# Strassen's block scheme for the up projections of two feed-forwards, with the feed-forward in two phases

## What is computed

```
def conv_ffn(h, w_up, conv_w, conv_b, w_down):
    u = h @ w_up                                  # 528x1024 @ 1024x5632
    up = jnp.pad(u, ((0, 0), (CONV_W - 1, 0), (0, 0)))
    c = conv_b + sum(up[:, j:j + Tp] * conv_w[j] for j in range(CONV_W))   # CONV_W = 3
    gate, val = jnp.split(c, 2, axis=-1)
    return (jax.nn.silu(gate) * val) @ w_down     # 528x2816 @ 2816x1024
h = h + conv_ffn(rms_norm(h, ln_ffn_g[i]), w_up[i], conv_w[i], conv_b[i], w_down[i])
```

## Time and profile before

| | |
|---|---|
| median of 3 runs (lowest, highest) | 2502.92 us (2499.54, 2505.1) |
| profiled execution: span, first to last instruction | 2497.3 us |
| PE, weight loads, DVE, ACT, POOL busy | 2391.5, 2135.3, 1371.9, 1060.1, 397.6 us |
| mean granted TensorE clock, as a share of full | 0.979 |
| `f0u`, `f0d` (us from the start) | 1375 to 1633, 1633 to 1762 |
| `f1u`, `f1d` | 2104 to 2362, 2362 to 2486 |

### The profile page before, as it was taken

The page is one execution under the profiler, slowest core; times in us unless marked ns, Lnnn a source line. Parts: engine busy times, 40 slices in busy tenths (PEclk is TensorE's granted clock), DMA queues, the critical chain, the costliest instruction groups (busy, mean ns, idle before and its releaser), DMA issues.

```text
span 2497.3 us, 41318 instructions
## 1 busy us (share of the span) xinstructions
PE 2391.5 (96%) x15443; PEld 2135.3 (86%) x15443; DVE 1371.9 (55%) x2095; ACT 1060.1 (42%) x1910; POOL 397.6 (16%) x350
## 2 busy tenths in 40 slices
PE   6999999999999999998989999999999989999998
PEld 5778777887899899887869999999888879999987
DVE  5896777223465245458745666643334445766621
ACT  5646764333343233324444333332455554333322
POOL 0000444700410100100121211100100002211100
PEclk8999999999999999999989999999999999999999
DMA  8563423332233353332102323323422122232332
GB/s 291 166 205 103 109 77 84 93 101 81 88 96 92 100 134 87 101 110 65 44 19 66 91 86 90 92 85 93 131 60 60 45 52 85 84 92 85 89 95 92
DMA packets 409481, 238.38 MB, mean 95 GB/s; under 512 B 11434, under 2 KB 400397, under 8 KB 409381
## 3 DMA queue, kind: packets, MB, share of 16 engines
q1 hardware_dynamic: 400549, 202.25, 28.8%
q0 software_dynamic: 8224, 32.61, 3.9%
q10 hardware_dynamic: 608, 2.16, 0.2%
HBM read 234.54 MB, written 5.00 MB: 96 GB/s over the span
## 4 chain that ended last, share of the span: by engine, by line
PE 81%; DVE 6%; ACT 5%; issue 4%; DMA 3%; POOL 0%; SPq 0%; ACTq 0%; DVEq 0%; POOLq 0%
PE PS L508 60%; PE PS L2056 6%; PE PS L1842 3%; DMA w_raw<-in_w_in_dram 2%; ACT w_hi L429 1%; PE PS L2092 1%; PE PS L1857 1%; PE PS L2187 1%; PE PS L1801 1%; DVE w_lo L435 1%; PE PS L1921 1%; PE PS L2134 1%; PE PS L1957 1%; PE PS L2071 1%; DVE conv_acc L2311 1%
## 5 line engine op out<-in xcount | busy, mean ns | idle before, releaser
L435 DVE TENSOR_TENSOR w_lo<-w_raw,w_hi 128x1024 fp32r<-128x1024 f32 (+2 forms) x376 | 470.4, 1251 | 628.4 <-ACT w_hi L429 627.3
L508 PE MATMUL PS<-op_hi,w_hi 128*128 128x264 f32 (+3 forms) x2440 | 600.9, 310 | 16.3 <-DVE w_lo L435 13.6
L508 PE MATMUL PS<-op_lo,w_hi 128*128 128x264 f32 (+3 forms) x2440 | 598.4, 309 | 0.0
L508 PE MATMUL PS<-op_hi,w_lo 128*128 128x264 f32 (+3 forms) x2440 | 595.8, 308 | 0.0
L429 ACT ACTIVATE w_hi<-w_raw 128x1024 fp32r<-128x1024 f32 (+2 forms) x376 | 378.9, 1008 | 314.0 <-PE PS L508 261.6
L508 PEld LDWEIGHTS PS<-op_hi,w_hi 128*128 128x128 f32 x2440 | 397.1, 189 | 47.7 <-DVE w_lo L435 16.3
L508 PEld LDWEIGHTS PS<-op_hi,w_lo 128*128 128x128 f32 x2440 | 396.7, 189 | 22.6
L508 PEld LDWEIGHTS PS<-op_lo,w_hi 128*128 128x128 f32 x2440 | 396.2, 189 | 21.9 <-issue 0.5
L508 PE MATMUL PS<-ff_hi,w_lo 128*128 128x512 f32 (+1 forms) x784 | 240.3, 343 | 0.0
L508 PE MATMUL PS<-ff_hi,w_hi 128*128 128x512 f32 (+1 forms) x784 | 239.9, 342 | 0.0
L508 PE MATMUL PS<-ff_lo,w_hi 128*128 128x512 f32 (+1 forms) x784 | 239.9, 342 | 0.0
(11 more groups left out here) (497 smaller groups left out, 3856.7 us busy)
## 6 DMA issues: line engine op xcount, KB each, us to landing
w_raw<-in_w_up_dram SPq DMA_DIRECT2D x120, 512.0 KB, 3.8
w_raw<-in_w_in_dram SPq DMA_DIRECT2D x64, 512.0 KB, 4.1
w_raw<-in_w_down_dram SPq DMA_DIRECT2D x64, 512.0 KB, 3.8
w_ada<-in_w_ada_dram POOLq DMA_DIRECT2D x12, 2048.0 KB, 9.0
decay<-sums_scratch SPq DMA_DIRECT2D x16, 512.0 KB, 5.2
w_raw<-in_w_branch_ssd_dram SPq DMA_DIRECT2D x16, 512.0 KB, 4.0
w_raw<-in_w_in_a_dram SPq DMA_DIRECT2D x16, 512.0 KB, 3.8
w_raw<-in_w_kv_b_dram SPq DMA_DIRECT2D x16, 512.0 KB, 3.9
```

What stands on the lines that cost most here:

```text
L435: dve.tensor_tensor(wlo[slot][:, 0:ks, :], wraw[slot][:, 0:ks, :], whi[slot][:, 0:ks, :].bitcast(F32), ALU.subtract).then_inc(sem("w_split ...
L508: last = pe.matmul(a[0:l.cols, h, 0:cn], w[slot][:, k, 0:l.cols], x[:, kk, c0:c0 + cn], start=(j == 0 and k == 0 and w is whi and x is l.h ...
```

## The change

The two `f{x}u` are replaced by a block scheme. A gate tile and a value tile of the weights form, with the two halves of the contraction (4 tiles each), a 2 by 2 block matrix; the activations form one with the contraction's halves and the token halves. The 8 block products become 7, each of 4 contraction tiles, 3 passes and 264 columns: 84 matmuls a pair. In exchange sums of blocks are formed. Of the activations this happens once a layer, in `to_feed_forward`: the second token half of `op_hi`, `op_lo` is now a difference of the halves, and there are three combined blocks `tx_val`, `tx_hi`, `tx_lo`. Of the weights it happens for every pair: POOL makes 4 sums (`fs_sum`), ACT 7 hi parts (`fs_hi`), DVE 7 lo parts (`fs_lo`). Sums of products are formed by ACT copying one PSUM bank into another before PE adds on to it, and by 2 additions on DVE.

Other parts of it: the feed-forward goes in phases of 12 and 10 tile pairs (`PHASE`), with a part of the down projection (`f{x}d0`, 12 contraction tiles; `f{x}d1`, 10) behind each; the first tap of the convolution moves from DVE to ACT, gate times value from DVE to POOL; after the last down projection DVE adds from PSUM, where ACT copied and POOL added. In the rest of the program some semaphores share a name; its work is the same.

```
+PHASE = 12
+        for ph in range(2):
+            L[f"f0d{ph}"] = Linear(plan, KD, down_src(I["w_down_2"][0], PHASE * ph), GHs[0], GLs[0],
+                                  kts=((8, 4), (8, 2))[ph], block1=False)
 # POOL, weights: four sums a pair
+            def fs_sums(x, t, par, i):
...
+                if not first:
+                    p = (5, 6, 7, 3)[i]
...
+                    pool.wait_ge(sem("fs_done"), fs_at(x, t, par, 7, place - 7))
+                if i == 0:
+                    pool.wait_ge(sem(f"fs_in{par}"), t * 32 + 32 * (NF // 2 * x + 1))
+                    a, b, op = raw[1][:, 0:4, :], raw[1][:, 4:8, :], ALU.add
+                elif i == 1:
...
+                    a, b, op = fs_sum[0][:], raw[0][:, 0:4, :], ALU.subtract
+                elif i == 2:
+                    a, b, op = raw[0][:, 0:4, :], raw[1][:, 0:4, :], ALU.subtract
+                else:
...
+                    a, b, op = raw[0][:, 4:8, :], fs_sum[1][:], ALU.subtract
+                pool.tensor_tensor(fs_sum[i][:], a, b, op).then_inc(sem("fs_sum"), 1)
 # POOL, one pair
+                def body(t, par, conv=True, ahead=True):
...
+                        fs_sums(x, nt, np_, 0)
+                        fs_sums(x, nt, np_, 1)
+                    if conv:
+                        gated(pt, pp)
+                    if ahead:
+                        fs_sums(x, nt, np_, 2)
+                        fs_sums(x, nt, np_, 3)
...
+                    scale(t, par, 0)
+                    scale(t, par, 1)
 # PE, one pair
+                    for p in (1, 5, 2, 6, 7, 3, 4) if first else (1, 5, 6, 2, 7, 3, 4):
+                        pe.wait_ge(sem("fs_lo"), fs_at(x, t, par, 7, FS_LO_NO[p]))
+                        if p in FS_SEED:
+                            pe.wait_ge(sem("fs_seed"), fs_at(x, t, par, 3, FS_SEED[p]))
...
+                        for k in range(4):
...
+                            for n, (w, v) in enumerate(((FS_HI[p], hi), (FS_HI[p], lo), (FS_LO[p][par], hi))):
+                                last = pe.matmul(acc, w[:, k, :], v[:, k, :], start=(p in (1, 5) and k + n == 0),
+                                                 stop=(k == 3 and n == 2), skip_group_check=True)
 # DVE, the lo part of product p's weights; one pair
+            def fs_lo(p, x, t, par):
+
+                dve.wait_ge(sem("fs_hi"), fs_at(x, t, par, 7, FS_HI_NO[p]))
+                if p in (5, 6, 2):
+                    dve.wait_ge(sem("fs_sum"), fs_at(x, t, par, 4, 2 if p == 5 else 4))
+                dve.tensor_tensor(FS_LO[p][par][:], fs_raw_of(p, par), FS_HI[p][:].bitcast(F32),
+                                  ALU.subtract).then_inc(sem("fs_lo"), 1)
 # DVE, operands, for each of the 8 residual tiles
+                    if g >= 4:
+                        k = g - 4
+                        link(dve.scalar_tensor_tensor(tv[:, 1, k, :], R[:, g, TH:T], gain(g), tv[:, 1, k, :], ALU.mult,
+                                                      ALU.subtract))
+                        link(dve.scalar_tensor_tensor(tv[:, 0, k, :], R[:, k, 0:TH], gain(k), tv[:, 1, k, :], ALU.mult,
+                                                      ALU.add))
+                        dve.scalar_tensor_tensor(tv[:, 2, k, :], R[:, g, 0:TH], gain(g), tv[:, 0, k, :], ALU.mult,
+                                                 ALU.subtract).then_inc(sem("fs_tv"), 1)
+                    if g >= 5:
+                        t_lo(g - 5)
+                    for p in {6: (1,), 7: (5,)}.get(g, ()):
+                        fs_lo(p, x, 0, 0)
```

More of the change, by code:

```diff
@@ L406, in halves, with load @@
             return ap.rearrange("p (a n) -> p a n", a=2)
-        def load(sp, l):
+        def load(sp, l, start=0):
             def body(g, t, par):
@@ L420, in load @@
             else:
-                pair_loop(sp, None, 0, l.groups, body)
+                for g in range(start, start + start % 2):
+                    body(g, g // 2, g % 2)
+                pair_loop(sp, None, start + start % 2, l.groups, body)
         def split_hi(act, l, t, par, j, ks=8):
@@ L492, in products_of @@
             cols = [(META, S)] if l.block1 else [(0, TH), (TH, TH)]
-            if l.hi is not HH and l.hi is not GH and l.block1:
+            if l.block1 and not any(l.hi is b for b in (HH, *GHs)):
                 cols = [(0, S)]
@@ L594, in late_sum @@
             return between
[L596 to L604, removed]
-            pair_loop(pool, None, 0, L[name].groups, body)
         def attn_gain(k):
@@ L928, in decay_rows, with fs_load @@
                 sp.dma_start(decay[i % 2][:], src).then_inc(sem(f"decay_in{i % 2}"), 16)
+            def fs_load(x, t, par):
+                w = I["w_up_2"][x].rearrange("(k p) n -> p k n", p=P)
+                first = isinstance(t, int) and t == 0
+                for u in range(2):
+                    if not first:
+                        if u:
+                            sp.wait_ge(sem("fs_lo"), fs_at(x, t - 1, par, 7, FS_LO_NO[4]))
+                        else:
+                            sp.wait_ge(sem("fs_done"), fs_at(x, t - 1, par, 7, FS_PLACE[2]))
+                    src = w[:, :, bass.ds(t * (2 * P) + (par * P + u * FF2), P)]
+                    sp.dma_start(fs_raw[par][u][:], src).then_inc(sem(f"fs_in{par}"), 16)
             for name, l in L.items():
@@ L1111, in _ @@
+            resid_sum_ff(0, "n4", L["oa2"])
+            for ph in range(2):
+                fs_pool(0, ph)
             link(pool.memset(stats[:], 1.0))
@@ L1513, in _, with fs_hi @@
-            feed_forward(0, "n4")
-            gained_hi(act, "n6", lambda k: attn_gain(KD + k), QHh, ("evacuated", L["f0d"].G0 + KD + 2))
+            def fs_hi(p, x, t, par):
+                if p in (1, 4):
+                    act.wait_ge(sem(f"fs_in{par}"), t * 32 + 32 * (NF // 2 * x + 1))
+                elif p != 2:
+                    act.wait_ge(sem("fs_sum"), fs_at(x, t, par, 4, FS_SUM[p] + 1))
+                act.activation(FS_HI[p][:], fs_raw_of(p, par), ACT.Copy).then_inc(sem("fs_hi"), 1)
@@ L2043, in project @@
+            for ph in range(2):
+                fs_pe(0, ph)
+                products(pe, L[f"f0d{ph}"], ("ff_ready", PHASE * ph))
             def project(g):
@@ L2244, in _ @@
             products(pe, L["ob2"], ("oB_ready", 4))
-            products(pe, L["f1u"], "n7_ready", between=late_sum(pe, "n7", 36))
-            products(pe, L["f1d"], ("ff_ready", NF))
+            for ph in range(2):
+                fs_pe(1, ph)
+                products(pe, L[f"f1d{ph}"], ("ff_ready", NF + PHASE * ph))
             for t in range(NT):
-                pe.wait_ge(sem("added"), ADDED["f1d"] + KD + 2)
+                pe.wait_ge(sem("evacuated"), L["f1d1"].G0 + KD + 2)
                 if t >= 2:
@@ L2717, in _ @@
+            to_feed_forward(0, L["oa2"], "n4")
+            fs_dve(0, 0)
+            down_add(L["f0d0"])
+            fs_dve(0, 1)
+            resid_lo(dve, "n5", L["f0d1"], kv_gain)
             for k in range(KD):
```

567 lines of the change are left out of this document (411 added, 156 removed).

## The result

Median of the changed kernel 2713.2 us (2709.1 to 2716.7), beside it 2503.1 us before (2499.5 to 2505.1): ratio 1.084, 95% interval 1.082 to 1.087, so 210 us slower. The profiled execution has a span of 2710.2 us, against 2497.3 before: +212.9. The forecast was 2661 in a range of 2592 to 2735: its direction and mechanism hold, and it is 52 us short.

A forecast was written before the change was run, and what follows sets the result against it. Exclusive use of DVE and POOL was to bound the up pairs at 14.9 us: +79.5 us a layer, +159 for both, -1.2 at the end, total +158; 2497.3 became 2655, plus 5.6 gave 2661 us, range 2592 to 2735.

The forecast's parts named there:

- Matmuls removed: Up projections: 84 matmuls a pair for 96, 1.47 us a pair, 64.7 us over 44 pairs; PE would need 10.3.
- Exclusive use: Up stages: two-SBUF-input DVE instructions and POOL exclude each other and set the pace; 2600 to 2700 us, chance 0.63.
- Rival E: Up stages: new POOL and DVE instructions run beside each other, PE sets the pace; 2461 us, chance 0.06.
- rival C: Up stages: each exclusive turn lasts the instruction's whole duration, 17.2 us a pair; 2744 us, chance 0.07.
- never overlapping by more than 0.15: Expected sign in the up stages: POOL's `fs_sum` and DVE's `fs_lo` rows overlap by at most 0.15 us.
- The sum of 14.3: Exclusive time per up pair: DVE 4.3 + 2.2, POOL 5.8 + 2.0, together 14.3 us.
- PE's waits: In each steady up pair PE waits once for product 6, about 3 us, and once for product 4, about 1.
- rival D: Up stages: PE's clock falls after waits; all of a pair at half speed takes 18.5 us; 2790 us, chance 0.08.
- Entry: After `oa2`: product 2 of pair 0 can start at 19 us, pair 0 ends at 32, pair 1 some 12 later.
- 10 x 14.9: Up part of phase 0: the ten pairs after the first two, each counted as steady at 14.9 us.
- Its down part, 12/22 of 129, plus 2 us: Phase 0's down part, per layer: 70.5 us, plus 2 us waited for the twelfth `ff_lo`.
- 2 + 58.5: Phase 1's down part, per layer: 2 us plus 58.5 us.

The follow-up runs named there:

- run 4: run 3 with POOL's two scalings and gate times value also cut to 8 columns and a memset each: 2500.2 us.
- run 2: The changed kernel with gate times value and the weight sums of the pairs ahead moved from POOL to DVE: 2657.5 us, ratio 1.061.
- run 3: The changed kernel with each of POOL's four weight sums replaced by an 8-column operation and two memsets: 2591.7 us.
- run 7: The kernel before, with plain eight products a pair, cut into phases of 12 and 10 pairs with equal down pieces: 2532.9 us, ratio 1.012.
- run 6: The changed kernel with down weights in equal pieces (6 + 6, 5 + 5 contraction tiles, not 8 + 4, 8 + 2): 2701.4 us, ratio 1.079.
- run 8: run 7 with each down weight piece split only over the columns it holds (768 or 640): 2519.7 us, ratio 1.007.

## Why the prediction was right, and where it was short

**Matmuls removed: right.** PE would need 10.3 us a pair; run 4 shows 10.18 with nothing in its way.

**Exclusive use: right as the cause, and shown.** Undone in part it gives back 56 us (run 2), without the sums 121 (run 3), without POOL's long reads 213 (run 4), with PE's instructions the same. Rival E, both engines beside each other, is out by the rows at 1508, and so is rival C, the rule of the Trainium skill (SBUF — State Buffer, "Who interferes with whom") that a turn lasts the whole instruction: the turns are 0.56, 0.98 and 1.18 where the durations alone are 0.68, 1.12 and 1.30. (C's 2744 also left out the 0.6 us a pair that the other sums add.) The sign "never overlapping by more than 0.15" holds for the turns alone: rows include the waiting, and those of `ff_lo` (1508.77) and the first scaling (1508.25) share 1.06 us.

**The sum of 14.3: mis-sized in one term.** From the ends of four pairs (1505.5 to 1567.2), each instruction charged with the time from the end of the one before it: 8 subtractions at 0.56 = 4.5 (forecast 4.3), two scalings at 0.98 = 2.0 (2.0), four sums at 1.18 and the gate at 1.19 = 5.9 (5.8), and four scalar_tensor_tensor at 0.70 = **2.8 for 2.2**. The 0.56 came from L2685 in the earlier trace rows, which had waited for POOL; here they mostly follow another DVE instruction or a link of 0.15 us and cost 0.68 and 0.77. Together 15.2, and 0.2 in which neither has its turn (forecast 0.6): 15.4 instead of 14.9 (15.25 and 15.55 in turn).

**PE's waits** are where they were forecast: some 3.4 us before product 6 (forecast 3), 1.1 or 0.1 before product 4 (1). TensorE is busy 71% of layer 1's first phase with its entry and 81% of the second, where some 70% were forecast.

**The clock, rival D:** it happens in part. In 22 of the 44 pairs, mostly every second one, product 6 runs at half clock behind its wait (up to 2.6 to 2.8 us instead of 1.57), so the windows show 0.91 to 0.93. Where such pairs take turns with the others, they are 0.3 us longer, and the wait of the next pair passes at full clock. The Trainium skill, TensorE: Matmul & The Clock Gate, section "HAM oscillation — how this bites in real kernels", tells of a fall in every tile; in this trace it is mostly every second pair. If the whole 0.3 us is its doing, which no run tested, it costs 6 to 7 us in all, where the forecast had nothing: a small part of the loss.

**Entry: nearly right, in part by luck.** Pair 0 ends 34.5 and 30.9 us after the last matmul of the output projection in layers 1 and 2 (forecast 32), pair 1 takes 11.9 and 12.3 (12). The DVE queue in layer 1 is longer than reckoned:

```profile
1377.51 1.56 DVE L2979 SCALAR_TENSOR_TENSOR tx_val<-resid,param_cols,tx_val 128x264 f32<-128x264 f32 x1
1379.11 1.40 DVE L2981 SCALAR_TENSOR_TENSOR tx_val<-resid,param_cols,tx_val 128x264 f32<-128x264 f32 x1
1380.54 0.49 DVE L2983 SCALAR_TENSOR_TENSOR tx_val<-resid,param_cols,tx_val 128x264 f32<-128x264 f32 x1
1380.95 0.98 DVE L2961 TENSOR_TENSOR tx_lo<-tx_val,tx_hi 128x792 fp32r<-128x792 f32 x1
...
1389.11 0.59 PE L2314 MATMUL PS<-op_hi,fs_hi 128*128 128x264 f32 x1 [9.24 <-DVE fs_lo L2951]
1396.26 0.59 PE L2314 MATMUL PS<-op_hi,fs_hi 128*128 128x264 f32 x1 [4.14 <-DVE fs_lo L2951]
```

The three linked instructions were put at 1.9 us; two of them stand behind POOL's sums and take 1.56 and 1.40, so a tile takes 6.5 to 7.1 us and not 5.0 plus 1.2. Product 2 still starts 19.3 us after the output projection (17.8 in layer 2), for a forecast of 19; but the terms that the prediction names, 24 less 11.7, a `tx_lo` and three `fs_lo`, add up to 15.4 and not to 19. TensorE's wait ahead of pair 0 is 9.2 and 7.7 us, where one of over 10 was forecast. What I did not have at all is that this begins inside the output projection: `oa2` lasts 26.0 us for 23.6, `ob2` 27.4 for 23.7.

**The third pair: a term that was not there.** "10 x 14.9" counts it as steady, but it takes 19.1 us in both layers. The down projection's first two weight pieces are split there, ahead of `fs_lo` 6 in DVE's queue and with a weight sum of POOL between them, and TensorE waits 6.6 us. The next pair takes 14.2 us, so that the two together cost 3.5 us a layer more than forecast:

```profile
1430.99 4.34 DVE L449 TENSOR_TENSOR w_lo<-w_raw,w_hi 128x1024 fp32r<-128x1024 f32 x2
...
1432.00 2.24 POOL L1210 TENSOR_TENSOR fs_sum<-fs_raw 128x512 f32<-128x512 f32 x1
...
1436.06 0.58 PE L2314 MATMUL PS<-tx_hi,fs_hi 128*128 128x264 f32 x1 [6.59 <-DVE fs_lo L2951]
```

**Down parts: the step that failed.** "Its down part, 12/22 of 129, plus 2 us" and "2 + 58.5": 133 us a layer. They take 143.7 and 139.1, +17 in all. I scaled TensorE's time by contraction tiles and took "the down parts as before", without asking what a shorter piece leaves for the split ahead of it: run 7 and its rows show that. In the change itself, TensorE waits 1.0 us for `w_lo` once in nearly every tile of the second down parts (a tile is 8.6 us; the expectation of run 6 says every second tile, which is not so):

```profile
1822.18 0.52 PE L522 MATMUL PS<-ff_hi,w_hi 128*128 128x264 f32 x2 [1.00 <-DVE w_lo L449]
1830.75 0.51 PE L522 MATMUL PS<-ff_hi,w_hi 128*128 128x264 f32 x2 [1.02 <-DVE w_lo L449]
```

**The balance of the 55 us** between +158 and +213: 17 from the down parts; 27 from the up parts, which took 694.3 us for 2 x 333.5 forecast (the third and fourth pairs are 7 of them, layer 1's entry 3, and most of the rest is 0.5 us in each of the 32 other steady pairs); 6 from `oa2` and `ob2`; 8 from the attention stages, where nothing was changed; less 2 to 3, because start and end are together 1.2 us shorter than forecast and the stages of before are 775.5 us long where the forecast took 774.

**What stays open:** why the untouched attention stage took 245.0 us at a clock of 0.90 here and 238.4 at 0.94 before. The same instructions took 236.1 to 245.1 us in the traces of the ten runs: 245.1 in run 2, 238.3 in run 3. The three kernels that keep the old up projection (before, runs 7 and 8) are among the four shortest, 236.1 to 238.4, and the nine others lie at 238.3 to 245.1, so part of it may come with the change. Where in its work the clock falls may be the cause, but no run tested that. It says how finely two traces can be compared as a whole: not under some 8 us.

## What to carry to other kernels

Before work is moved to an idle engine, ask what it shares with the busy one: add up, per turn of the loop, the time in which only one of DVE (with two SBUF inputs) and POOL (reading SBUF) can work, from the ends of neighbouring rows, and hold that sum against TensorE's time, not each engine's busy share. An algorithm with an eighth fewer products must find its additions free: here 12 saved matmuls (1.5 us) asked for four weight sums and three more subtractions on a pair of engines with 4 us to spare. And when a stage is cut in two, the time that a weight piece leaves for the split ahead of it shrinks with the piece; look for what stands in that queue.
